# A two-layer trunk on one core: forget gates turned to rows of heads, an earlier load of decay rows, and an output projection that begins among the last attention units

## The chip, the core and the metric

The kernel runs on one core of one Trainium2 chip. The metric is the device time of one execution in microseconds, as the median of several runs. Five engines work side by side and are kept in step by semaphores that the program sets and waits for: TensorE (matrix products and transposes), VectorE, ScalarE, GpSimd (POOL) and SyncE (SP). SP, ScalarE and GpSimd also issue transfers, each from a queue of its own in the order of its program.

## What is computed

The input is 512 positions of width 1024 in float32. There are two layers. The change touches the part between them and the attention of the second one:

```python
def shared_kv(x_kv, kv_norm, kv_w, kv_b_f, k_norm):
    h = rmsnorm(x_kv, kv_norm)
    kvf = h @ kv_w                       # 1024 -> 1024 keys, 1024 values, 16 forget logits
    k, v, f = jnp.split(kvf, [D_MODEL, 2 * D_MODEL], axis=-1)
    k = rmsnorm(k.reshape(B, S, N_HEADS, HEAD_DIM), k_norm)
    v = v.reshape(B, S, N_HEADS, HEAD_DIM)
    log_f = jax.nn.log_sigmoid((f + kv_b_f).astype(jnp.float32))
    cum = jnp.cumsum(log_f, axis=1).transpose(0, 2, 1)
    return k, v, cum

def forgetting_attention(h, k, v, cum, w_qg, q_norm, w_out):
    q, gate = jnp.split(h @ w_qg, 2, axis=-1)
    q = rmsnorm(q.reshape(B, S, N_HEADS, HEAD_DIM), q_norm)
    # per block of 128 queries: scores q k^T * scale + cum[query] - cum[key], causal, softmax, times v
    return (o * jax.nn.sigmoid(gate)) @ w_out
```

There are 16 heads of width 64. Before this stands layer 0 (a gated mixer and a mixture of 32 experts), after it the second mixture of 32 experts, whose weights (6 MB each) stream in from memory.

## The kernel before

**Order of the work.** The second half of the program runs: normalised rows "kv" are turned and split; key projection (G_K, 8 groups); forget logits; value projection (G_VV, 8 groups); rows "b" are turned; cumulative sums; query projection (G_Q, 8 groups); 32 attention units (8 pairs of heads times 4 blocks of 128 queries); output projection (G_WO, 8 groups); router; mixture of experts (`moe_pe`, `moe_dve`, `moe_act`, `moe_loads`). Each engine has its own program, written out by hand, and runs it strictly in order.

**Products.** A float32 value is written as the sum of two rounded parts, hi and lo. `split_product` makes three matmuls of 128 x 128 by 512: hi x hi, hi x lo, lo x hi (L1203, L1204, L1205 of the profile). A group is 8 blocks of the inner dimension, so 24 matmuls, accumulated in one of the banks `ps[0]` and `ps[1]` in turn. A weight tile is loaded by SP (`load_tile`, which waits until the tile two before has been used), its hi part is made by ScalarE (L583), its lo part by VectorE (L795), four pieces each. Products of plain float32 operands are made without splitting; the profile shows two matmul instructions for each of those, and one for a transpose.

**Forget logits.** For each block of 128 positions, each of 8 inner blocks and both parts, two plain float32 products with 64 stationary columns and 16 moving ones (L1520). VectorE adds the bias (L1103), ScalarE makes log-sigmoid from it, VectorE joins the pieces (L1116). The layout is positions on partitions, `lf[128, 4 * 16]`.

**Cumulative sums.** Ten products of 16 moving columns with a triangle or ones as stationary operand (L1535, L1536), copied by VectorE (L1125), turned to 16 rows of heads by four transposes (L1540), negated by ScalarE and stored to memory as `ncum_rows`.

**Decay rows.** In the scores, each unit needs the row of its head on all 128 partitions. ScalarE loads them in pairs (`load_nck`, L713) from `ncum_rows` into two slots of `nck`, the first two when the last query block has been written (`kn_out` 16). VectorE adds them to the scores and takes the maximum in one instruction (L1147).

**Attention units.** In turn `u` TensorE makes the scores of unit u (L1557, mask L1560) into banks 2 * (u % 2) and the next, a slice of the gate projection (L1572, which for the first pair waits for a sum that VectorE makes, L1137), the product with values of the pair that is complete (L1585, once in four units, 3 units late), and the transposes of the probabilities of unit u - 2 (L1596). VectorE copies these out (L1166, ScalarE the other head, L744), and after the product with values it applies the gate and splits the result (L1172 to L1174). Units 32 to 34 of the loop only finish what is begun.

**Output projection.** It waits for the gated result of all 8 pairs, then makes 8 groups: n = 0, 1 (512 output columns each) by t = 0 to 3. Group g uses bank g % 2; from the third on it waits for VectorE's addition of group g - 2 (`x_attn`, L1180). VectorE's order is: add group 0, split the second weight tile, add group 1, and so on. SP loads expert weights as groups end: three parts after the last product with values, two after group 4, four after group 8.

Of the kernel before, what the change touches and what calls it, by code (L numbers as in the profile page):

```python
# [24 lines left out]
P = 128  # L25
D = 1024
T = 512
# [30 lines left out]
def trunk(nc, x_in, a_norm, a_w_in, a_b_in, a_v_norm, a_w_s, a_b_s, a_w_out, kv_norm, kv_w, kv_b_f, k_norm,  # L58
          b_norm, b_w_qg, q_norm, b_w_out, m_norm, m_w_group, m_b_group, m_w_expert, m_b_expert,
          m_w1, m_w3, m_w2, out):  # L60
    with ExitStack() as ctx:
# [68 lines left out]
        nck = scr(6 * COL, 10 * COL).rearrange("p (b h n) -> p b h n", b=2, h=2)  # L130
# [59 lines left out]
        cols_raw = sb("cols_raw", [N_COLS, P])  # L190
# [5 lines left out]
        wf = sb("wf", [P, KD, HEADS])  # L196
# [88 lines left out]
        kn_out = sem("kn_out")  # L285
        f_done = sem("f_done")
        f_ready = sem("f_ready")
# [3 lines left out]
        cum_ready = sem("cum_ready")  # L291
        cumT_done = sem("cumT_done")
        ncum_ready = sem("ncum_ready")
        ncum_stored = sem("ncum_stored")
        nck_loaded = sems("nck_loaded", 2)
        s_done = sem("s_done")
# [140 lines left out]
        def _(pool):  # L437
# [105 lines left out]

            item_tables(1)

        @block.scalar
        def _(act):
# [150 lines left out]
            head_norms(0, G_K, 0, KT, {0: T_K + 1, 5: T_VV})  # L698
            act.wait_ge(f_ready, 1)
# [3 lines left out]
            split_tile(T_VV + 1)  # L703
            split_tile(T_Q)
            transposed_rows("b")
            act.wait_ge(cumT_done, 1)
# [4 lines left out]
            def load_nck(c):  # L711
                for h in range(2):
                    act.dma_start(nck[:, c % 2, h, :], ncum_rows[2 * c + h].partition_broadcast(P))\  # L713
# [5 lines left out]
            load_nck(0)  # L719
# [31 lines left out]
        def _(dve):  # L751
# [262 lines left out]

            dve.wait_ge(small_loaded, 32)
# [65 lines left out]
            def head_norms(r, g0, splits):  # L1081
                for j in range(8):
# [13 lines left out]
                    if j in splits:  # L1096
# [4 lines left out]
            dve.wait_ge(f_done, 1)  # L1101
            f3 = lf[:, 0, :].rearrange("p (t n) -> p t n", t=NT)
            v.tensor_tensor(f3, ps[6][:, 0:NT * HEADS].rearrange("p (t n) -> p t n", t=NT),  # L1103
                            over_t(bf_bc[:, :], HEADS), ALU.add).then_inc(f_ready, 1)
            dve.wait_ge(f_ready, 1)
            then(v.tensor_scalar(lf[:, 2, :], lf[:, 0, :], 0.0, None, ALU.min))
            for j in range(8):
# [6 lines left out]
                if j == 3:  # L1114
# [15 lines left out]
            for u in range(n_units + 4):  # L1130
                if u < n_units:
# [7 lines left out]
                    if i == 0:  # L1139
                        dve.wait_ge(nck_loaded[c % 2], 32 * (c // 2 + 1))  # L1140
                    for h in range(2):
                        dve.wait_ge(s_done, 2 * u + h + 1)
                        if u >= 3:
# [4 lines left out]
                                               in1=nck[:, c % 2, h, 0:w], scale=-1.0, scalar=BIG, op0=ALU.add,  # L1148
# [44 lines left out]
        def _(pe):  # L1193
# [75 lines left out]
            def project(i, g0, bank_free):  # L1269

                for t in range(NT):
# [5 lines left out]
                    last.then_inc(acc_ready, 1)  # L1277

# [151 lines left out]
            nc.tensor.transpose(ps[6][:, 0:N_COLS], cols_raw[:, :], ident[0:N_COLS, 0:N_COLS])\  # L1430
# [94 lines left out]
            project(T_VV, G_VV, free_vv)  # L1525
# [112 lines left out]
```

## Time and profile before

| | us |
|---|---|
| median of 3 runs | 1659.6 |
| lowest and highest | 1659.26 and 1671.69 |
| span of the profiled execution, first to last instruction | 1656.1 |
| TensorE busy (share of the span) | 1513.8 (91%) |
| VectorE busy | 982.5 (59%) |
| ScalarE busy | 458.7 (28%) |
| GpSimd busy | 24.7 (1%) |

The page gives busy time by engine, the granted TensorE clock in slices of the span (1.00 is 2.4 GHz, 0.50 is 1.2 GHz), the costliest groups of instructions, the transfers, and the chain of work that ended last, followed back from the last instruction. TensorE's busy time is no measure of how much it does: a product at the lower clock is busy about twice as long.

### The profile page before, as it was taken

What the parts mean: (1) busy time and instruction counts of PE and PEld (TensorE: products, weight loads), DVE (VectorE), ACT (ScalarE), POOL (GpSimd) and SP (SyncE); (2) the same over time, 40 slices, a digit from 0 to 9 for tenths busy, and PEclk for the clock granted to TensorE, in tenths of its full rate; (3) what the DMA queues carried; (4) which work ended last, traced back from release to release, by engine and by line L of the source; (5) the groups of instructions that cost most, each with busy time, mean ns of one, the idle gap of its engine ahead of it and who ended that gap; (6) DMA issues with size and microseconds to landing.
All of it is one profiled execution on the core that took longest, in us unless ns stands there. A gap on an engine that the chain in (4) does not pass through costs nothing.

```text
span 1656.1 us, 45993 instructions
## 1 busy us (share of the span) xinstructions
PE 1513.8 (91%) x19125; PEld 1019.5 (62%) x19126; DVE 982.5 (59%) x2067; ACT 458.7 (28%) x757; POOL 24.7 (1%) x61
## 2 busy tenths in 40 slices
PE   8999999998999899977899989989999999977667
PEld 7888888755555555544787844457655555543334
DVE  5337642576776677745625346651776777754446
ACT  5442321422222122211541334433221222211111
POOL 2100000100000000000000000000000000000000
PEclk9999999999999999988989999999999999998888
DMA  5421224889999999999122121143899997999995
GB/s 206 131 102 51 102 102 152 332 361 411 418 415 425 429 429 404 431 427 390 35 81 95 59 89 56 60 191 126 363 412 427 424 402 299 404 426 428 429 429 211
DMA packets 55787, 462.17 MB, mean 279 GB/s; under 512 B 4433, under 2 KB 4561, under 8 KB 31153
## 3 DMA queue, kind: packets, MB, share of 16 engines
q1 hardware_dynamic: 51680, 453.00, 66.6%
q10 hardware_dynamic: 2480, 4.75, 0.9%
q0 software_dynamic: 1568, 3.59, 0.7%
q8 instruction: 44, 0.72, 0.2%
q14 instruction: 15, 0.11, 0.0%
HBM read 459.19 MB, written 2.13 MB: 279 GB/s over the span
## 4 chain that ended last, share of the span: by engine, by line
PE 60%; DMA 33%; DVE 4%; issue 1%; SPq 1%; ACT 0%; DVEq 0%; ACTq 0%
DMA EB<-in_m_w 32%; PE ps L1345 10%; PE ps L1203 9%; PE ps L1205 9%; PE ps L1204 9%; PE ps L1334 5%; PE ps L1355 4%; PE ps L1317 3%; PE ps L1572 3%; PE ps L1557 1%; PE ps L1585 1%; PE ps L1596 1%; PE ps L1444 1%; DVE EB_r L795 1%; SPq L384 1%
## 5 line engine op out<-in xcount | busy, mean ns | idle before, releaser
L1345 PE MATMUL ps<-EB,SCR 128*32 128x256 f32 x6016 | 378.4, 408 | 95.1 <-DMA EB<-in_m_w 81.6
L1345 PEld LDWEIGHTS ps<-EB,SCR 128*32 128x32 f32 x6016 | 200.7, 117 | 265.1 <-issue 144.1
L914 DVE TENSOR_TENSOR X<-X,ps 128x1024 f32 x188 | 221.1, 1218 | 28.1 <-PE ps L1317 28.1
L1205 PE MATMUL ps<-EB_r 128*128 128x512 f32 x512 | 201.7, 394 | 0.0
L1334 PE MATMUL ps<-H,SCR 128*32 128x256 f32 x3072 | 185.7, 382 | 0.0
L906 DVE TENSOR_TENSOR SCR<-SCR,ps 128x128 f32<-128x128 f32 x94 | 37.2, 395 | 248.4 <-ACT SCR L621 248.3
L1355 PE MATMUL ps<-EB,SCR 128*32 128x256 f32 x3008 | 179.5, 379 | 0.0
L624 ACT ACTIVATE SCR_r<-ps,SCR 128x256 f32 x94 | 44.6, 474 | 445.4 <-PE ps L1355 445.4
L1355 PEld LDWEIGHTS ps<-EB,SCR 128*32 128x32 f32 x3008 | 97.8, 110 | 64.5
L1317 PEld LDWEIGHTS ps<-SCR_r 32*128 32x128 f32 x3136 | 101.4, 187 | 48.1 <-issue 44.5
L1203 PE MATMUL ps<-EB_r,H_r 128*128 128x512 f32 x320 | 127.9, 400 | 1.0 <-DVE EB L993 1.0
L1317 PE MATMUL ps<-SCR_r 32*128 32x256 f32 x3136 | 121.3, 292 | 8.0 <-DVE SCR_r L927 3.8
L1334 PEld LDWEIGHTS ps<-H,SCR 128*32 128x32 f32 x3072 | 90.0, 109 | 62.2
L1204 PE MATMUL ps<-EB_r,H_r 128*128 128x512 f32 x320 | 126.0, 394 | 0.0
L1204 PE MATMUL ps<-EB_r 128*128 128x512 f32 x320 | 125.2, 391 | 0.0
L621 ACT ACT_TABLE_LOAD x94 | 120.6, 1283 | 2.0 <-ACT SCR L617 0.3
L795 DVE TENSOR_TENSOR EB_r<-EB,EB_r 128x1024 fp32r<-128x1024 f32 x80 | 92.9, 1220 | 42.0 <-ACT EB_r L583 42.0
L1205 PEld LDWEIGHTS ps<-EB_r 128*128 128x128 f32 x512 | 97.2, 190 | 20.7
L621 ACT ACTIVATE SCR<-ps 128x128 f32<-128x128 f32 x94 | 26.1, 278 | 281.9 <-PE ps L1345 281.9
L583 ACT ACTIVATE EB_r<-EB 128x1024 fp32r<-128x1024 f32 x80 | 78.2, 1047 | 72.9 <-DMA EB<-in_a_w_out 41.8
L890 DVE SCALAR_TENSOR_TENSOR SCR_r<-SCR,item_slot,SCR_r 128x256 fp32r<-128x256 f32 x196 | 86.3, 482 | 15.4 <-DVE SCR_r L887 15.3
L1203 PE MATMUL ps<-EB_r 128*128 128x512 f32 x192 | 76.6, 399 | 2.0 <-DVE EB_r L1174 2.0
(233 smaller groups left out, 1643.6 us busy)
## 6 DMA issues: line engine op xcount, KB each, us to landing
EB<-in_m_w SPq DMA_DIRECT2D x192, 2048.0 KB, 9.9
EB<-in_a_w_in SPq DMA_DIRECT2D x8, 2048.0 KB, 9.0
EB<-in_a_w_out SPq DMA_DIRECT2D x4, 2048.0 KB, 7.8
EB<-in_kv_w SPq DMA_DIRECT2D x4, 2048.0 KB, 14.4
EB<-in_b_w_qg SPq DMA_DIRECT2D x4, 2048.0 KB, 8.9
SCR<-ncum_rows ACTq DMA_DIRECT2D x16, 256.0 KB, 3.7
EB<-in_b_w_out SPq DMA_DIRECT2D x2, 2048.0 KB, 9.4
X<-in_x SPq DMA_DIRECT2D x4, 512.0 KB, 7.0
```

What stands on the lines that cost most here:

```text
L583: a.activation(ring_hi[j][:, 2 * q:2 * q + 2, :], ring[j][:, 2 * q:2 * q + 2, :], ACT.Copy)\
L621: a.activation(silu, ps[0][:, 0:P], ACT.Silu).then_inc(m["silu"], 1)
L795: v.tensor_tensor(ring_lo[j][:, 2 * q:2 * q + 2, :], ring[j][:, 2 * q:2 * q + 2, :], ring_hi[j][:, 2 * q:2 * q + 2, :].bitcast(F32), ALU.s ...
L890: v.scalar_tensor_tensor(dst[:, i, :], toks[1], item_slot[:, bass.ds(items[i] + 2, 1)], dst[:, i, :].bitcast(F32), ALU.is_equal, ALU.add). ...
L914: add = v.tensor_tensor(X_t, X_t, moved[1][:, :, t, :], ALU.add)
L1203: mm(o, left[0], right[0], start=start, stop=False)
L1204: mm(o, left[0], right[1], start=False, stop=False)
L1205: return mm(o, left[1], right[0], start=False, stop=stop)
L1317: last = mm(moved[banks][:, g, t, :], sides[rows, i, t * P:(t + 1) * P], y_parts[rows, i, k, :], start=i == 0 and k == 0, stop=i == 1 and ...
L1334: last = mm(ps[1][g * CAP:(g + 1) * CAP, 0:CW], S[:, c, :], H[:, c * D + g * CW:c * D + (g + 1) * CW], start=c == 0, stop=c == NT - 1)
L1345: last = mm(ps[0][g * CAP:(g + 1) * CAP, 0:2 * P].rearrange("p (w n) -> p w n", w=2), xT[:, k, :], w13_sb[s][:, :, k, g * P:(g + 1) * P], ...
L1355: last = mm(ps[2][g * CAP:(g + 1) * CAP, CW:2 * CW], hidT[:, c, :], w2_sb[s][:, c, g * CW:(g + 1) * CW], start=c == 0, stop=c == KE - 1)
```

## The change

1. **Logits with heads on partitions.** Instead of 128 plain products with 16 moving columns, 24 split products with the 16 gate weights as stationary operand and all 512 positions as moving one. The gate weights are split once, early in layer 0 (ScalarE, VectorE). ScalarE copies the [16, 512] result out; TensorE turns it back to positions on partitions with four transposes after the second group of the value projection; VectorE adds the bias then, and joins the pieces after the fifth group rather than the fourth.
2. **Sums with heads on partitions.** The same ten products with the operands exchanged: the logs are the stationary operand (16 columns), the triangle or ones the moving one (128 columns). The result has heads on partitions at once; VectorE's copy, the four transposes and their semaphores are gone.
3. **First pair's decay rows.** GpSimd loads them into `gain`, after the sums are stored and the last rows "b" are written. ScalarE no longer loads them; the even slot of `nck` is now `gain` for all even pairs.
4. **Output projection.** In loop turns 32, 33 and 34 TensorE makes blocks 0 to 2, 3 to 5 and 6 of group 0; after the loop blocks 0 to 6 of group 1; then block 7 of both, and the other groups as before.

```diff
-        nck = scr(6 * COL, 10 * COL).rearrange("p (b h n) -> p b h n", b=2, h=2)
+        nck = [at.rearrange("p (h n) -> p h n", h=2) for at in (gain[:, :], scr(6 * COL, 8 * COL))]
...
+            pool.wait_ge(ncum_stored, 16)
+            pool.wait_ge(norm["b"]["hrow"], NT)
+            for h in range(2):
+                pool.dma_start(nck[0][:, h, :], ncum_rows[h].partition_broadcast(P)).then_inc(nck_first, 16)
+
             item_tables(1)
...
             act.wait_ge(wst_ready, 2)
+            act.wait_ge(col_loaded, 16 * N_COL_LOADS)
+            a.activation(wf_hi[:, :, :], wf[:, :, :], ACT.Copy).then_inc(wf_split, 1)
...
             head_norms(0, G_K, 0, KT, {0: T_K + 1, 5: T_VV})
+            act.wait_ge(f_done, 1)
+            a.activation(junk[0:HEADS, 0:T], ps[6][0:HEADS, :], ACT.Copy).then_inc(f_out, 1)
+            split_tile(T_VV + 1)
             act.wait_ge(f_ready, 1)
...
-            load_nck(0)
             load_nck(1)
...
+            dve.wait_ge(wf_split, 1)
+            v.tensor_tensor(wf_lo[:, :, :], wf[:, :, :], wf_hi[:, :, :].bitcast(F32), ALU.subtract).then_inc(wf_split, 1)
...
+                if j == 1:
+                    dve.wait_ge(f_turned, 1)
+                    v.tensor_tensor(f3, ps[7][:, 0:NT * HEADS].rearrange("p (t n) -> p t n", t=NT),
+                                    over_t(bf_bc[:, :], HEADS), ALU.add).then_inc(f_ready, 1)
+                    dve.wait_ge(f_ready, 1)
+                    then(v.tensor_scalar(lf[:, 2, :], lf[:, 0, :], 0.0, None, ALU.min))
+                if j == 4:
...
-            dve.wait_ge(cum_done, 1)
-            v.tensor_copy(lf[:, 1, :], ps[7][:, 0:NT * HEADS]).then_inc(cum_ready, 1)
...
-                        dve.wait_ge(nck_loaded[c % 2], 32 * (c // 2 + 1))
+                        dve.wait_ge(*((nck_loaded[c % 2], 32 * (c // 2 + c % 2)) if c else (nck_first, 32)))
...
-            for t in range(NT):
-                for k in range(KD):
-                    for part, h in enumerate(h_part(k, t)):
-                        for c in range(2):
-                            last = mm(ps[6][c * HALF:(c + 1) * HALF, t * HEADS:(t + 1) * HEADS],
-                                      h.bitcast(F32)[:, c * HALF:(c + 1) * HALF], wf[:, k, :],
-                                      start=k == 0 and part == 0, stop=k == KD - 1 and part == 1)
+            pe.wait_ge(wf_split, 2)
+            for k in range(KD):
+                last = split_product(ps[6][0:HEADS, :], (wf_hi[:, k, :], wf_lo[:, k, :]), h_part(k), k == 0, k == KD - 1)
             last.then_inc(f_done, 1)
+
+            def turn_forget():
+
+                pe.wait_ge(f_out, 1)
+                for t in range(NT):
+                    last = nc.tensor.transpose(ps[7][:, t * HEADS:(t + 1) * HEADS], junk[0:HEADS, t * P:(t + 1) * P],
+                                               ident[0:HEADS, 0:HEADS])
+                last.then_inc(f_turned, 1)
...
             pe.wait_ge(lf_ready, 1)
-            for c in range(NT):
-                o = ps[7][:, c * HEADS:(c + 1) * HEADS]
-                for b in range(c):
-                    mm(o, ones[:, :], lf[:, 0, b * HEADS:(b + 1) * HEADS], start=b == 0, stop=False)
-                last = mm(o, tri_in[:, :], lf[:, 0, c * HEADS:(c + 1) * HEADS], start=c == 0, stop=True)
+            for t in range(NT):
+                o = ps[6][0:HEADS, t * P:(t + 1) * P]
+                for b in range(t):
+                    mm(o, lf[:, 0, b * HEADS:(b + 1) * HEADS], ones[:, :], start=b == 0, stop=False)
+                last = mm(o, lf[:, 0, t * HEADS:(t + 1) * HEADS], tri_in[:, :], start=t == 0, stop=True)
             last.then_inc(cum_done, 1)
...
+            def attend_out(n, t, c0, c1):
+
+                i, g = T_WO + n, NT * n + t
+                if c0 == 0:
+                    pe.wait_ge(*((x_attn, g - 1) if g >= 2 else (s_max, 2 * (PAIRS * NT - 1))))
+                for c in range(c0, c1):
+                    if n == 0 and t == 0:
+                        pe.wait_ge(o_gated, c + 1)
+                    if n == 1:
+                        router_step(1, t, c)
+                    wait_split(i, c, t == 0)
+                    last = split_product(ps[g % 2][:, :], (GT_hi[:, c, t * P:(t + 1) * P], GT_lo[:, c, t * P:(t + 1) * P]),
+                                         w_part(i % 2, c), c == 0, c == PAIRS - 1)
+                if c1 == PAIRS:
+                    last.then_inc(acc_ready, 1)
...
+                if u >= n_units:
+                    attend_out(0, 0, 3 * (u - n_units), min(3 * (u - n_units) + 3, PAIRS - 1))
                 if 2 <= u < n_units + 2:
...
-            pe.wait_ge(o_gated, PAIRS)
...
+            attend_out(0, 1, 0, PAIRS - 1)
+            for t in range(2):
+                attend_out(0, t, PAIRS - 1, PAIRS)
+            for g in range(2, 2 * NT):
+                attend_out(g // NT, g % NT, 0, PAIRS)
             router_end(1)
```

## Rows read from the trace of the kernel before

**Rows 1.** The page: shares of the span in the chain that ended last.

```profile
PE 60%; DMA 33%; DVE 4%; issue 1%; SPq 1%; ACT 0%; DVEq 0%; ACTq 0%
```

**Rows 2.** Stretches: us, busy time by engine, then granted clock, DMA share, GB/s.

```profile
852.50:857.80 5.30, 5.30 (x105) 5.26 (x103) 0.00 (x0) 0.00 (x0) 0.00 (x0) 0.51 0.48 177
...
904.00:910.60 6.60, 4.11 (x33) 3.37 (x32) 5.97 (x8) 3.39 (x7) 0.00 (x0) 1.00 0.77 258
...
913.90:917.30 3.40, 3.40 (x10) 2.69 (x9) 0.00 (x0) 0.59 (x1) 0.00 (x0) 0.52 0.06 14
...
966.10:972.00 5.90, 5.85 (x16) 2.45 (x16) 0.02 (x1) 1.28 (x1) 0.00 (x0) 0.50 1.04 377
...
1099.00:1108.40 9.40, 7.38 (x26) 4.41 (x27) 1.81 (x3) 3.90 (x4) 0.00 (x0) 0.68 0.66 242
...
1128.20:1157.00 28.80, 28.46 (x217) 23.13 (x215) 5.89 (x13) 13.93 (x16) 0.00 (x0) 1.00 0.37 147
```

**Rows 3.** Timeline of TensorE, logits to value projection: start, us, line, count, [idle before].

```profile
847.88 0.29 PE L1520 MATMUL ps<-wf,H_r 128*64 128x16 f32 x4
...
857.76 1.12 PE L1479 MATMUL ps<-ident,SCR 128*128 128x128 f32 x4
858.53 0.78 PE L1203 MATMUL ps<-EB_r,H_r 128*128 128x512 f32 x1
...
862.91 0.40 PE L1204 MATMUL ps<-EB_r,H_r 128*128 128x512 f32 x1
```

**Rows 4.** Timeline of TensorE around the cumulative sums.

```profile
910.74 0.29 PE L1536 MATMUL ps<-lf,tri_in 128*128 128x16 f32 x2
...
913.36 0.60 PE L1540 MATMUL ps<-ident,lf 128*16 128x128 f32 x4 [0.32 <-DVE lf L1125]
913.72 0.49 PE L1203 MATMUL ps<-EB_r,H_r 128*128 128x512 f32 x1
```

**Rows 5.** Chain that ended last, at the first attention unit: start, us, what.

```profile
966.55 5.40 DMA SCR<-ncum_rows
```

**Rows 6.** Timeline of TensorE at the first two attention units.

```profile
971.88 0.36 PE L1560 MATMUL ps<-mask_b,ident_b 128*128 128x128 bf16 x2
973.68 0.70 PE L1572 MATMUL ps<-H,EB 128*128 128x512 f32 x1 [1.44 <-DVE H L1137]
```

**Rows 7.** Timeline of TensorE, last attention units and output projection.

```profile
1087.36 2.37 PE L1585 MATMUL ps<-EB 128*64 128x512 f32 x16
...
1092.98 0.60 PE L1596 MATMUL ps<-ident,SCR 128*128 128x128 f32 x4
1094.01 1.02 PE L1596 MATMUL ps<-ident,SCR 128*128 128x128 f32 x6 [0.42 <-DVE EB L1166]
1097.25 1.06 PE L1596 MATMUL ps<-ident,SCR 128*128 128x128 f32 x8 [2.22 <-DVE EB L1166]
1099.05 3.71 PE L1585 MATMUL ps<-EB 128*64 128x512 f32 x16 [0.73 <-DVE EB L1166]
1104.73 0.50 PE L1203 MATMUL ps<-EB_r 128*128 128x512 f32 x1 [1.97 <-DVE EB_r L1174]
...
1117.33 0.39 PE L1203 MATMUL ps<-EB_r 128*128 128x512 f32 x1
...
1128.21 0.39 PE L1203 MATMUL ps<-EB_r 128*128 128x512 f32 x1
```

**Rows 8.** Timeline of VectorE in the same stretch.

```profile
1096.56 0.55 DVE L1166 COPY EB<-ps 128x384 f32<-128x384 f32 x1
...
1112.09 0.69 DVE L1180 TENSOR_TENSOR X<-X,ps 128x512 f32<-128x512 f32 x1 [7.42 <-PE ps L1205]
1112.70 4.63 DVE L795 TENSOR_TENSOR EB_r<-EB,EB_r 128x1024 fp32r<-128x1024 f32 x4
```

**Rows 9.** Timeline of SP's queue during the output projection.

```profile
1128.40 28.61 SPq L370 DMA_DIRECT2D EB<-in_m_w  x3
```

**Rows 10.** Transfers by line: queue, count, KB each, median us to landing.

```profile
EB<-in_a_b_s POOLq DMA_DIRECT2D x1, 512.0 KB, 8.5
```

More of the change, by code:

```diff
@@ L189, in trunk @@
         eps = sb("eps", [P, 1])
-        cols_raw = sb("cols_raw", [N_COLS, P])
+        cols_raw, wf_hi_rows = sb_split("cols_raw", [P, P])
+        wf_hi = wf_hi_rows[:, :].rearrange("p (k n) -> p k n", k=KD)
         cols = sb("cols", [P, N_COLS])
@@ L195, in trunk @@
         gpk = sb("gpk", [P, 2, KD])
-        wf = sb("wf", [P, KD, HEADS])
+        wf, wf_lo = sb_split("wf", [P, KD, HEADS])
         bf_bc = sb("bf_bc", [P, HEADS])
@@ L285, in trunk @@
         kn_out = sem("kn_out")
+        wf_split = sem("wf_split")
         f_done = sem("f_done")
+        f_out = sem("f_out")
+        f_turned = sem("f_turned")
         f_ready = sem("f_ready")
@@ L295, in trunk @@
         nck_loaded = sems("nck_loaded", 2)
+        nck_first = sem("nck_first")
         s_done = sem("s_done")
@@ L1267, in router_end, with project @@
                 router_logits(l, NT - 1)
-            def project(i, g0, bank_free):
+            def project(i, g0, bank_free, between=None):
                 for t in range(NT):
@@ L1277, in project @@
                     last.then_inc(acc_ready, 1)
+                    if between is not None and t == 1:
+                        between()
             def project_transposed(i, g0, bank_free):
@@ L1531, in _ @@
             pe.wait_ge(lf_ready, 1)
-            for c in range(NT):
-                o = ps[7][:, c * HEADS:(c + 1) * HEADS]
-                for b in range(c):
-                    mm(o, ones[:, :], lf[:, 0, b * HEADS:(b + 1) * HEADS], start=b == 0, stop=False)
-                last = mm(o, tri_in[:, :], lf[:, 0, c * HEADS:(c + 1) * HEADS], start=c == 0, stop=True)
-            last.then_inc(cum_done, 1)
-            pe.wait_ge(cum_ready, 1)
-            for c in range(NT):
-                last = nc.tensor.transpose(ps[6][0:HEADS, c * P:(c + 1) * P], lf[:, 1, c * HEADS:(c + 1) * HEADS],
-                                           ident[:, :])
-            last.then_inc(cumT_done, 1)
+            for t in range(NT):
[3 more added lines that the diff above has]
+                last = mm(o, lf[:, 0, t * HEADS:(t + 1) * HEADS], tri_in[:, :], start=t == 0, stop=True)
+            last.then_inc(cum_done, 1)
             project_heads("b", T_Q, G_Q, 1, free_q)
             turn_heads(15)
+            def attend_out(n, t, c0, c1):
[12 more added lines that the diff above has]
+                    last.then_inc(acc_ready, 1)
             pe.wait_ge(kn_out, 16)
@@ L1598, in _ @@
                         last.then_inc(pt_tr, 1)
-            pe.wait_ge(o_gated, PAIRS)
-            for n in range(2):
-                i = T_WO + n
-                for t in range(NT):
-                    g = G_WO + 4 * n + t
-                    if 4 * n + t >= 2:
-                        pe.wait_ge(x_attn, 4 * n + t - 1)
-                    for c in range(PAIRS):
-                        if n == 1:
-                            router_step(1, t, c)
-                        wait_split(i, c, t == 0)
-                        last = split_product(ps[g % 2][:, :], (GT_hi[:, c, t * P:(t + 1) * P],
-                                                               GT_lo[:, c, t * P:(t + 1) * P]),
-                                             w_part(i % 2, c), c == 0, c == PAIRS - 1)
-                    last.then_inc(acc_ready, 1)
+            attend_out(0, 1, 0, PAIRS - 1)
[3 more added lines that the diff above has]
+                attend_out(g // NT, g % NT, 0, PAIRS)
             router_end(1)
```

19 lines of the change are left out of this document (5 added, 14 removed).

## The prediction

> **What bounds the kernel now.** I read the page's chain first. TensorE carries 60% of the span, transfers 33% [rows 1]; nearly all of the transfers are expert weights of the two mixture stages, which the change does not touch. So a microsecond counts where TensorE is the chain, and I read the stretches that the diff names in the order of time: granted clock by stretch, then TensorE's own timeline around each. The reader is to see four places. The forget logits, 256 narrow instructions, run without a pause, yet during them the granted clock falls from full to the lower level, 1.2 GHz, and stays there into the value projection [rows 2, 3]. Around the sums over positions TensorE waits a little, and the query projection starts at the lower clock [rows 2, 4]. At the first attention unit the chain holds 5.40 us of the decay rows' transfer, and TensorE stands 1.44 us behind VectorE [rows 5, 6]. At the last units it stands 0.42, 2.22, 0.73 and 1.97 us, and its clock is down again until 1108.4, when ten products of the output projection are through [rows 2, 7].
>
> Does time won there reach the end? The next expert loads wait in SP's queue for TensorE: the three SP issues of 1128.40 stretch over 28.61 us, since the last of them waits for the last projection group, and the transfer engines are 0.37 busy from 1128.2 to 1157.0 [rows 2, 9]. The weights of the second mixture stage are thus asked for when the projection is done, not when a full queue lets them, and everything behind it moves as one.
>
> A full-clock product of 512 columns costs 0.227 us here: 48 of them lie between 1117.33 and 1128.21 [rows 7].
>
> **Forget logits.** From their first instruction (847.88) to the eleventh product of the value projection (862.91) pass 15.03 us [rows 3]: 256 narrow instructions, one turn of key heads (857.76 to 858.53) and ten products at the lower clock (858.53 to 862.91). After: three products for each of 8 blocks, 24 x 0.227 = 5.44; the turn at twice the clock, half of 0.77 = 0.39; ten products at full clock, 2.27; and, two groups on, four transposes back, at the 0.115 of a narrow instruction below, 0.46. That makes 8.56, a gain of **6.5**. I take the cost of a 16-wide stationary block as that of a 128-wide one, which is the dearer neighbour; no row has it for a 512-column product. What is queued behind: ScalarE copies the logits out and splits the next weight tile, whose load was issued in time; VectorE waits for the turned logits after the second value group, TensorE does not want its next split before the fifth, 2 x 5.44 us later. The new split of the gate weights (one small instruction on ScalarE, one on VectorE, in the first layer) is taken at nothing: TensorE is then inside a group of 24 products, 5.4 us, and only wants VectorE's next result two groups on. Uncovered it would cost under 1 us. Bounds for this part: 6.5, or less 3.3 if the clock falls all the same (below).
>
> **Sums over positions.** Before, the first product starts at 910.74, TensorE waits 0.32 us at 913.36 for VectorE's copy, does four transposes, and the query projection starts at 913.72: 2.98 us [rows 4]. The 20 instructions until that wait took 913.36 - 0.32 - 910.74 = 2.30, or 0.115 each. After, 20 instructions with the operands exchanged, no copy, no transposes: 2.30. Each moves 128 columns instead of 16, and loads 16 instead of 128; I price them alike. Gain 0.68. From 913.9 to 917.3 the products ran at 0.52 of the clock; the same work at full clock is done in half the 3.4 us. Is that 1.7 won? At 904 to 910.6 TensorE was busy only 4.11 of 6.6 us with transposes of 128 columns and kept a clock of 1.00; both falls, here and at 852.5, came behind runs of 16-column instructions [rows 2, 3, 4], and neither run remains. I take it: together **2.4**, bounds 0.7 and 2.4.
>
> The Trainium skill (TensorE: Matmul & The Clock Gate, Part 1: The HAM clock gate) has the clock go down after the array was idle. By it this 1.7 would stay lost, for the pauses between 904 and 910.6 remain, and the sum would come out 1.7 us less. The trace does not agree at the forget logits, where the clock fell to 0.51 with TensorE busy 5.30 of 5.30 us [rows 2].
>
> **First decay rows.** Before, ScalarE asks for them only when queries are done. After, GpSimd's queue asks as soon as the sums are stored. The slowest small load on that queue in this trace took 8.5 us [rows 10]; two in a row would be there 17 us after 914, by 931, and the first reader wants them at 967. The cover is the whole query projection, some 36 us. What is won is not 5.40: VectorE is freed 4 to 5 us earlier, but TensorE, at the lower clock (0.50 from 966.1 to 972), has own work until 972.2, and stood only 1.44 us for VectorE before 973.68 [rows 2, 6]. After that TensorE sets the pace of the units. Gain **1.4**. Bounds: 0, if VectorE is late for another reason; 3, if the clock rises sooner. The GpSimd issue is behind nothing and its next customer is the mixture stage. The slot in `gain` is free once the last normalised rows of "b" are written, before 910.
>
> **Projection among the last units.** I lay it out from the rows [rows 7, 8]. TensorE is free at about 1093.5. Nine products (blocks 0 to 2 of group 0): 2.04, to 1095.55. Six transposes, which began at 1094.01 before, now end at about 1096.2; VectorE takes them at 1096.56 as before, because it is busy with other work until then. So nothing is lost here. Nine products (blocks 3 to 5), to 1098.25; the last eight transposes thus start 1.0 later than at 1097.25. From there to the last value products it was 1.80, so these start at 1100.05, at full clock now since no pause over 0.8 is left, and take 2.3 (the same sixteen at 1087.36), to 1102.35; before, 1102.76. Then 3 + 21 products, 5.44, to 1107.8; VectorE's gate of the last pair, 1.97 after the value products, is ready at 1104.3 and hidden. Six more products, 1.36, to 1109.15.
>
> Here the change adds a wait: the third group needs the bank of the first, and group 0 ends only three products before group 1. Its last product is out at 1108.65, VectorE's addition takes 0.69 (1112.09), so the third group starts at 1109.4, 0.25 late. Behind that addition VectorE splits the last weight tile, 4.63, and only then adds group 1: 1114.7. The fourth group wants that at 1109.4 + 5.44 = 1114.85. It just fits; were it late, each tenth counts. Two groups more, 10.88: the fifth starts at 1120.3 instead of 1128.21, a gain of **7.9**. Bounds: 4.5 if the clock falls as before (1.4 on the value products, ten products at 0.2 more each), 8.2 without the new wait.
>
> **Sum.** 6.5 + 2.4 + 1.4 + 7.9 = 18.2 us. The profiled execution spans 1656.1 us; that gives 1637.9. The median of the runs is 1659.6, 3.5 more, which lies around the span and stays. Forecast **1641.4 us**.
>
> **Rivals.**
> 1. *The clock falls under the new product as well.* Only 16 columns of the array hold weights, and no row shows such a run. If it fell after 4.6 us as now (847.88 to 852.5), four products cost 0.2 more each, the turn 0.39 and ten products 2.1: 3.3 us. With the 1.7 of the sums: 18.2 - 5.0 = 13.2, 1646.4 us; with the last units at the lower clock too (3.4 us) 1649.8. For it: the falls of [rows 2]. Against: 512-column products come without a pause.
> 2. *Only the query projection starts slow.* For it the 2.5 us of pauses before 910.6; against it the 1.00 held through them. 18.2 - 1.7 = 16.5, 1643.1 us. This is what the skill's rule above gives.
> 3. *The expert loads do not come sooner.* If transfers in flight were the limit behind the projection, most of the gain would be given back: about 1656. Against it the 0.37 of [rows 2].
> 4. *Slower: GpSimd's loads are late.* One wait, VectorE's for the first pair. Up to 967.4 a late landing costs nothing, until about 972 it eats the 1.4, from there each microsecond costs one; with the other gains (16.8) the kernel is slower than before once they land after about 989, over 70 us after their issue, against 8.5 seen. Landing at 995 they would make it 1659.6 - 16.8 + 23 = 1666 us.
> 5. *Luck with the clock.* It rises sooner at the first units: 1637 to 1639 us.
>
> The Trainium skill (SBUF — State Buffer, SBUF: two separate sides) warns that GpSimd cannot write its descriptors while VectorE runs certain copies within SBUF. It speaks for rival 4; no row shows such a delay, and I have no price for it beyond the 8.5 us.
>
> **How the numbers follow.** The forecast 0.50, with its own range of 1639.5 to 1643.5; rival 1 0.20, rival 2 0.15, rival 3 0.04, rival 4 0.03, rival 5 0.08. Leaving out 3 and 4 and the far ends of 1 and 5, the range is 1638 to 1649. A change of 1%, 16.6 us, is about what a measurement of this kernel tells from none; the border is 1643.0. Below it lie four fifths of the forecast (0.40), half of rival 2 (0.08) and rival 5 (0.08): faster 0.56. Slower is rival 4: 0.03. Within 1%: 0.41.
>
> **What would show it.** Right: the logits as 24 products over 5.4 us, clock 1.0 through the value projection's start; the query projection at 0.227 from its first products; VectorE's first reduction about 0.5 us behind the mask product, released by TensorE; the fifth output group some 18 us earlier; a wait of about 0.25 us ahead of the third. Wrong: a clock of 0.5 in any of the first three, a load of `gain` from GpSimd as what ends VectorE's wait, a long wait of TensorE for VectorE's addition in the fourth group, or the wait for expert weights after 1186 longer by what was won.

## The result, and the profile after

The changed kernel takes 1638.15 us (median of four runs, 1635.26 to 1647.78), the kernel before 1661.55 in the same rounds (1659.26 to 1671.69): a ratio of 0.9871, with an interval from 0.9837 to 0.9905. In later rounds it took 1641.18 us (1637.96 to 1645.70, six runs) against 1658.22 (1651.81 to 1664.53, eleven runs), 0.9906 [0.9879, 0.9932]. Faster, then, by 1.3% in the first rounds and 0.9% in the second, about 20 us in the mean of the two differences (23.4 and 17.0). Executions of one kernel lie up to 12.5 us apart in the first rounds, which matters for everything below.

The profiled execution spans 1636.7 us, 19.4 less than that of before. The four places, in the order of time. Stretches of the kernel after, as in [rows 2] (length, busy time of TensorE, its weight loads, VectorE, ScalarE and GpSimd, then granted clock, transfer share, GB/s):

```profile
848.70:855.03 6.33, 6.33 (x34) 3.10 (x32) 1.58 (x3) 1.48 (x3) 0.00 (x0) 1.00 0.80 263
855.03:859.50 4.47, 4.47 (x23) 3.68 (x22) 0.00 (x0) 3.72 (x5) 0.00 (x0) 1.00 0.27 97
899.30:908.20 8.90, 6.41 (x53) 5.20 (x51) 8.02 (x12) 4.33 (x8) 0.00 (x0) 1.00 0.69 238
908.20:911.00 2.80, 2.80 (x14) 2.27 (x13) 0.00 (x0) 0.59 (x1) 0.15 (x1) 1.00 0.05 12
959.10:965.00 5.90, 5.87 (x16) 2.46 (x17) 1.65 (x5) 2.16 (x5) 0.00 (x0) 0.50 0.81 296
1084.50:1093.90 9.40, 8.67 (x54) 6.48 (x52) 4.74 (x11) 3.97 (x8) 0.00 (x0) 1.00 0.62 225
1093.90:1101.00 7.10, 7.05 (x31) 5.51 (x30) 2.50 (x5) 2.44 (x3) 0.00 (x0) 1.00 0.88 330
1101.00:1112.30 11.30, 11.25 (x50) 9.31 (x51) 5.86 (x7) 0.00 (x0) 0.00 (x0) 1.00 0.82 349
```

The clock is 1.00 at the logits and into the value projection (before 0.51), at the start of the query projection (before 0.52) and at the last units (before 0.68). Only the first attention unit still runs at 0.50.

The timeline of TensorE in the kernel after, at the same places (start, length, line, count, idle time before it):

```profile
849.06 0.48 PE L1214 MATMUL ps<-H_r,cols_raw_r 128*16 128x512 f32 x1
...
854.67 0.60 PE L1492 MATMUL ps<-ident,SCR 128*128 128x128 f32 x4
855.03 0.48 PE L1214 MATMUL ps<-EB_r,H_r 128*128 128x512 f32 x1
...
905.96 0.39 PE L1554 MATMUL ps<-tri_in,lf 128*16 128x128 f32 x2
...
908.25 0.50 PE L1214 MATMUL ps<-EB_r,H_r 128*128 128x512 f32 x1
...
964.86 0.39 PE L1589 MATMUL ps<-mask_b,ident_b 128*128 128x128 bf16 x2
965.05 2.15 PE L1601 MATMUL ps<-H,EB 128*128 128x512 f32 x4
...
1091.56 2.37 PE L1614 MATMUL ps<-EB 128*64 128x512 f32 x16 [0.73 <-DVE EB L1177]
...
1100.56 0.39 PE L1216 MATMUL ps<-EB_r 128*128 128x512 f32 x1
1101.05 0.50 PE L1214 MATMUL ps<-EB_r 128*128 128x512 f32 x1
```

The logits are 24 products from 849.06 to 854.67, 5.61 us, where 256 instructions had taken 9.88 [rows 3]. The sums go from 905.96 to 908.25, 2.29 us against 2.98 [rows 4]. Ahead of the second unit there is no pause where 1.44 stood [rows 6]. The waits of 0.42, 2.22 and 1.97 at the end are gone [rows 7]; 0.73 is left, and the new wait stands ahead of the third output group: the last product is issued at 1100.56 and runs for some 0.23, the next starts at 1101.05.

VectorE and GpSimd at the first decay rows, and VectorE and SP at the output projection, in the kernel after:

```profile
910.85 1.07 POOL L550 DMA_DIRECT2D gain<-ncum_rows  x2 [104.42 <-DMA ncum_rows<-SCR]
...
960.30 0.29 DVE L1158 CUSTOM_DVE_ANT_0 SCR<-ps,gain 128x128 f32<-128x128 f32 x1 [1.53 <-PE ps L1589]
...
1100.31 0.69 DVE L1191 TENSOR_TENSOR X<-X,ps 128x512 f32<-128x512 f32 x1 [4.47 <-PE ps L1216]
1100.92 4.62 DVE L806 TENSOR_TENSOR EB_r<-EB,EB_r 128x1024 fp32r<-128x1024 f32 x4
1105.46 0.68 DVE L1191 TENSOR_TENSOR X<-X,ps 128x512 f32<-128x512 f32 x1
...
1112.26 28.64 SPq L373 DMA_DIRECT2D EB<-in_m_w  x3
```

The loads were asked for at 910.85 and the transfer list gives them 3.4 us each; VectorE's first reduction waits for TensorE, not for them. The weights of the second mixture are asked for at 1112.26, 16.14 earlier than in [rows 9].

### The profile page after: what moved, and what is told of

It is laid out like the page before. It is cut to its first block, busy times and chain, and to the rows that moved or that the text cites. A ratio compares the mean times of both kernels' runs of the same rounds, so it can differ in the third digit from the quotient of the medians.

```text
span 1636.7 us, 45535 instructions
## 1 busy us (share of the span) xinstructions
PE 1499.2 (92%) x18893; PEld 1007.2 (62%) x18894; DVE 982.1 (60%) x2067; ACT 459.3 (28%) x759; POOL 25.8 (2%) x63
## 3 DMA queue, kind: packets, MB, share of 16 engines
q10 hardware_dynamic: 2192, 4.23, 0.8%
## 4 chain that ended last, share of the span: by engine, by line
PE 67%; DMA 26%; DVE 4%; issue 1%; SPq 0%; ACT 0%; DVEq 0%
DMA EB<-in_m_w 26%; PE ps L1358 12%; PE ps L1214 9%; PE ps L1216 9%; PE ps L1215 9%; PE ps L1347 6%; PE ps L1368 6%; PE ps L1330 4%; PE ps L1601 3%; PE ps L1586 1%; PE ps L1614 1%; PE ps L1627 1%; PE ps L1210 1%; PE ps L1457 1%; PE ps L1237 1%
## 5 line engine op out<-in xcount | busy, mean ns | idle before, releaser
L925 DVE TENSOR_TENSOR X<-X,ps 128x1024 f32 x188 | 221.1, 1218 | 28.7 <-PE ps L1330 28.7
```

The lines of the kernel that those rows point to most:

```text
L925: add = v.tensor_tensor(X_t, X_t, moved[1][:, :, t, :], ALU.add)
```

## The trace cut into stretches

One execution against another hides a term of 2 us under a spread of 8. So each profile was cut at instructions that all kernels have, and the lengths compared, in us:

- **A**: turn of key heads ahead of the logits, to the first transposes of the rows of "b"
- **B**: from there to the tenth product of the query projection
- **C**: first scores of the first attention unit to those of the fifth
- **D**: transposes behind the scores of the last unit, to SP's issue behind the fourth output group
- **start** is what lies before A, **end** the second mixture behind the last output group. Their code is the same in all, but for the small split of the gate weights

| kernel | start | A | B | C | D | end |
|---|---|---|---|---|---|---|
| before | 847.35 | 56.83 | 13.25 | 16.32 | 35.42 | 499.04 |
| after | 848.70 | 50.60 | 11.14 | 14.88 | 27.73 | 495.77 |
| a_logits | 847.51 | 50.60 | 12.97 | 18.83 | 32.49 | 496.02 |
| b_sums | 844.20 | 55.30 | 11.12 | 18.36 | 37.61 | 497.64 |
| c_rows | 845.78 | 56.83 | 16.17 | 14.23 | 35.65 | 501.26 |
| d_out | 848.22 | 56.82 | 16.11 | 17.91 | 27.74 | 494.95 |
| undo_sums | 843.55 | 50.60 | 14.68 | 14.60 | 27.74 | 499.61 |
| undo_decay | 848.58 | 50.60 | 11.11 | 19.57 | 27.74 | 497.13 |
| tail_fill | 850.44 | 55.27 | 15.99 | 18.66 | 34.49 | 496.34 |
| fill_wide | 849.40 | 50.60 | 11.12 | 11.92 | 27.73 | 496.56 |
| fill_narrow | 843.39 | 50.60 | 11.11 | 14.47 | 27.74 | 499.65 |
| before_again | 855.37 | 55.27 | 16.01 | 18.15 | 35.63 | 499.36 |
| after_again | 845.72 | 50.60 | 11.14 | 14.40 | 27.74 | 498.41 |
| fill_wide_again | 845.04 | 50.60 | 11.14 | 11.91 | 27.74 | 499.78 |

In the pair of profiles the local gains are 6.23 (A), 2.11 (B), 1.44 (C) and 7.69 (D), 17.5 in all. The start and the end of the same code vary by 12.0 and 6.3 us over the table: the rest of the 19.4 is the end, 3.27 shorter, less 1.35 of a later start. The end is no shorter with the earlier projection in the mean (497.7 us over the eight profiles that have it, 498.3 over the six others), so both are put down to the spread between executions. What lies between the stretches differs little: 48.7 to 49.2 us from B to C, 110.5 from C to D (111.1 in c_rows), 28.7 from D to the end.

## Each part alone

The kernel before with one part of the change each, three rounds beside the kernel before (1659.86 us, 1652.16 to 1672.81, 31 runs).

**a_logits**, the logits as rows of heads (the lines of code shown here and below are shortened):

```diff
-for t, k, part, c: mm(ps[6][...], h[...], wf[:, k, :])
+for k in range(KD):
+    last = split_product(ps[6][0:HEADS, :], (wf_hi[:, k, :], wf_lo[:, k, :]), h_part(k), ...)
```

> The kernel before with the first part alone: split product for the forget logits, turned back after the second value group. Theory (by content): the stretch from the turn ahead of the logits to the first transposes of the rows b falls from 56.8 us to 50.6, the clock stays at 1.00 through the start of the value projection, and the query projection still starts at about half the clock, because the sums are the old narrow ones. Rival (luck): the clock falls under the 16-wide product in this execution, the stretch is 53 to 54 us. Whole kernel: 6.2 us less than before.

Measured 1652.72 us (1648.42 to 1665.17, 10 runs), 0.9974 [0.9944, 1.0003]. A is 50.60, and the value projection starts at full clock. The query projection still starts at the lower clock, as expected (0.50 from 908.4 to 911.7).

**b_sums**, the sums with exchanged operands, without copy and transposes:

```diff
-mm(o, tri_in[:, :], lf[:, 0, c * HEADS:(c + 1) * HEADS], ...)
+mm(o, lf[:, 0, t * HEADS:(t + 1) * HEADS], tri_in[:, :], ...)
```

> The kernel before with the exchanged operands of the cumulative sums alone. Theory (the old clock falls come from runs of 16-column instructions): the old logits lose the clock again, at about 4.6 us from their start; the query projection starts at full clock, the stretch from the transposes of rows b to the tenth query product goes from 13.25 us to 11.1. Rival (the Trainium skill, TensorE: Matmul & The Clock Gate, Part 1: The HAM clock gate: the clock goes down after idleness, and the pauses among the transposes remain): that start stays slow, 12.6 us. Whole kernel: 2.1 us less, or 0.7.

Measured 1656.05 us (1653.53 to 1662.42), 0.9974 [0.9950, 0.9999]. B is 11.12, and the clock is 1.00 at the start of the query projection, though the logits are still narrow and brought it down in A, some 6 us behind their start rather than the 4.6 expected. The clock was at 1.00 through the transposes too, in this one profile, so the rival of the expectation did not come true.

**c_rows**, the first pair's decay rows loaded by GpSimd into `gain`:

```diff
-            load_nck(0)
+pool.dma_start(nck[0][:, h, :], ncum_rows[h].partition_broadcast(P)).then_inc(nck_first, 16)
```

> The kernel before with the first decay rows loaded by GpSimd into gain alone. Theory: VectorE starts its first reduction 4.6 us sooner, but from the first scores to those of the fifth unit only 1.4 us are won, 16.3 to 14.9, as TensorE's own work at the lower clock takes the place. Rival: the whole 4 to 5 us, 11.5. Whole kernel: 1.4 us less.

Measured 1657.59 us (1647.25 to 1663.62), 0.9979 [0.9949, 1.0010]. C is 14.23, where 14.9 was expected, and VectorE's first reduction starts 1.17 us behind the first scores instead of 5.83.

**d_out**, the output projection among the last units:

```diff
+                if u >= n_units:
+                    attend_out(0, 0, 3 * (u - n_units), min(3 * (u - n_units) + 3, PAIRS - 1))
```

> The kernel before with the earlier output projection alone. Theory: from the transposes of unit 29 to the issue behind the fourth output group 35.4 us become 27.7, clock 1.00 throughout, 0.25 us of wait ahead of the third group. Rival: the gain depends on the other parts (their clock), less than 5 us here. Whole kernel: 7.7 us less, and the mixture stage behind it as long as before (499.0) within what it varies by.

Measured 1650.89 us (1647.38 to 1656.25), 0.9941 [0.9918, 0.9963]. D is 27.74.

By medians the four give 7.1, 3.8, 2.3 and 9.0 us, 22.2 together, which agrees with the 23.4 and 17.0 of the whole within what times of whole executions leave open. The whole-kernel times can't rank them, and for a_logits and c_rows they don't even establish a gain, since the intervals reach past 1. The stretches can: each part brings its own stretch to the same length with and without the others, so none needs another. A part in its new form takes the same time in every profile, to 0.03 us in A, B and D. In its old form it does not, and that is the finding that the next sections follow.

## What the profile of before had shown cheaply

**undo_sums**, the changed kernel with the old sums, one execution:

```diff
-mm(o, lf[:, 0, t * HEADS:(t + 1) * HEADS], tri_in[:, :], ...)
+mm(o, tri_in[:, :], lf[:, 0, c * HEADS:(c + 1) * HEADS], ...)
```

> The changed kernel with the cumulative sums alone put back (narrow instructions, VectorE's copy, four transposes). Theory: from the transposes of rows b to the tenth query product 11.1 us go back to 12.8 to 13.3, with the clock near half behind the sums. Rival (the falls were chance): the clock stays at 1.00 and it is 11.8.

Measured 1640.57 us, B 14.68: 3.5 more than the changed kernel's, where the profile of before had shown only 2.1 more, and past the 12.8 to 13.3 that were expected. The clock is 1.00 up to 901.9 and 0.50 from there to 905.0; the first narrow sum had begun at 900.72.

**undo_decay**, the changed kernel with the old load of the first pair's rows, one execution:

```diff
-                        dve.wait_ge(*(... if c else (nck_first, 32)))
+                        dve.wait_ge(nck_loaded[c % 2], 32 * (c // 2 + 1))
+            load_nck(0)
```

> The changed kernel with the first pair's decay rows loaded as before, by ScalarE behind the query heads. Theory 1 (the late rows make a pause that also brings the clock down a second time): first to fifth unit 17 to 19 us against 14.2 to 14.9, VectorE waits for the transfer 5 to 6.6 us, time about 1641. Theory 2 (only the 1.44 us pause of the first profile): 16.0 to 16.4 us, time about 1640.

Measured 1644.60 us, C 19.57, 4.7 to 5.3 more than with the early load and a little more than the 17 to 19 of theory 1. Its TensorE and VectorE at the first units:

```profile
963.76 1.14 PE L1581 MATMUL ps<-EB 64*128 64x256 f32 x4
964.83 0.29 PE L1584 MATMUL ps<-mask_b,ident_b 128*128 128x128 bf16 x2
968.45 3.48 PE L1596 MATMUL ps<-H,EB 128*128 128x512 f32 x4 [3.33 <-DVE H L1143]
971.87 0.92 PE L1581 MATMUL ps<-EB 64*128 64x384 f32 x4
...
972.84 1.94 PE L1596 MATMUL ps<-H,EB 128*128 128x512 f32 x4
...
966.75 0.29 DVE L1153 CUSTOM_DVE_ANT_0 SCR<-ps,SCR 128x128 f32<-128x128 f32 x1 [8.13 <-DMA SCR<-ncum_rows]
```

VectorE waits 8.13 us for the rows (5 to 6.6 expected), TensorE stands 3.33 for VectorE. The four products behind that pause take 3.48 us, the same four a little later 1.94. The clock had risen by 965 and went down a second time:

```profile
959.20:962.00 2.80, 2.80 (x9) 1.55 (x10) 0.00 (x0) 0.96 (x1) 0.00 (x0) 0.50 1.02 390
962.00:966.00 4.00, 3.12 (x9) 0.88 (x7) 0.00 (x0) 0.33 (x1) 0.00 (x0) 0.66 0.72 257
966.00:970.00 4.00, 1.55 (x2) 0.84 (x3) 3.21 (x13) 1.97 (x8) 0.00 (x0) 0.76 0.03 13
970.00:974.00 4.00, 4.00 (x12) 1.39 (x11) 1.83 (x6) 0.42 (x1) 0.00 (x0) 0.81 0.00 0
974.00:978.70 4.70, 4.57 (x18) 1.87 (x16) 4.25 (x15) 2.88 (x10) 0.00 (x0) 1.00 0.03 3
```

So late rows cost a pause and a second spell at 1.2 GHz. In the profile of before the pause was 1.44 and no second spell came; in the five other profiles with the old load the pause was 1.83 to 3.06 and a second spell came each time.

**before_again**, the kernel before once more, nothing edited:

> The kernel before once more, for a second set of stretches. Theory 1 (the profile of before shown first has by chance short stretches behind the sums and at the first units): sums to tenth query product about 15 to 16 us against 13.25, first to fifth unit about 18 against 16.32. Theory 2 (those two are what this kernel always takes, and only the kernels with one part changed differ): 13.25 and 16.32 within 0.3.

Measured 1669.96 us, span 1668.1. B is 16.01 and C 18.15 against 13.25 and 16.32. Its last transposes and first sum, its stretches around the sums, and those at the first units:

```profile
916.20 1.94 PE L1226 MATMUL ps<-ident,SCR 128*128 128x128 f32 x8 [1.23 <-DVE EB_r L787]
917.94 0.45 PE L1536 MATMUL ps<-lf,tri_in 128*128 128x16 f32 x2
...
910.60:914.00 3.40, 2.13 (x19) 1.89 (x18) 2.91 (x4) 2.06 (x4) 0.00 (x0) 1.00 0.56 140
914.00:918.00 4.00, 2.77 (x17) 2.45 (x16) 3.89 (x7) 1.73 (x3) 0.00 (x0) 0.71 1.03 395
918.00:922.20 4.20, 4.20 (x21) 4.12 (x20) 1.34 (x2) 0.60 (x1) 0.00 (x0) 0.50 0.03 11
...
979.00:983.00 4.00, 2.38 (x8) 0.48 (x6) 1.18 (x5) 0.85 (x4) 0.00 (x0) 0.80 0.68 216
983.00:987.00 4.00, 3.48 (x6) 1.16 (x8) 2.85 (x9) 1.12 (x5) 0.00 (x0) 0.62 0.00 0
```

Here too the clock goes down a second time in C (0.80, then 0.62). And in B it was down before the first 16-column sum was issued, among the transposes with their pauses of 1.27 and 1.23. The prediction laid the fall in B to the narrow sums; this one came without them.

**after_again**, the changed kernel once more, nothing edited:

> The changed kernel as it is, timed in more rounds beside the next one. Expected: 1638 us, span 1635 to 1640; turn ahead of the logits to the first transposes of rows b 50.60, those to the tenth query product 11.1, first unit to fifth 14.2 to 14.9, transposes of the last unit but two to the issue of the next weights 27.73. If the new stretches only happened to be alike so far, one of them comes out over 0.5 us apart.

Measured as told at the top, span 1636.2: 50.60, 11.14, 14.40, 27.74. The new stretches hold.

Mean lengths over all profiles with a stretch in its old and in its new form:

| | old form | new form | gain | predicted |
|---|---|---|---|---|
| A | 56.05 (6 profiles, 55.27 to 56.83) | 50.60 (8) | 5.5 | 6.5 |
| B | 15.03 (7, 12.97 to 16.17) | 11.13 (7) | 3.9 | 2.4 |
| C | 18.26 (7, 16.32 to 19.57) | 14.52 (5, 14.23 to 14.88) | 3.7 | 1.4 |
| D | 35.36 (5, 32.49 to 37.61) | 27.74 (8) | 7.6 | 7.9 |

(C in its new form counts fill_narrow and leaves out the kernels with wide fillers; D in its old form leaves out tail_fill.) The sum is 20.7 us, in agreement with the 23.4 and 17.0 of the medians.

## What the clock is worth at the last units

**tail_fill**, the kernel before with 16 unread instructions of 128 columns in each of two of the pauses, one execution:

```diff
+                if u >= n_units:
+                    keep_busy(0, (8, 8, 0)[u - n_units])
```

> The kernel before, with 8 products of 128 x 128 by 128 columns that nobody reads put into the loop turns 32 and 33, where the change puts its output products; the output projection itself is left where it was. It shows the part of the gain that is only clock. Theory: the last product with values takes 2.4 us instead of 3.7 and the output projection starts at full clock, so that the stretch of 35.4 us loses 3.3, 32.1; the other 4.4 of the 7.7 are work moved into pauses. Rival: the fillers hold up the transposes and nothing is won, 35 or more.

Measured 1661.33 us, D 34.49, only 0.9 under the mean of the old form: neither the 32.1 of the theory nor the 35 of the rival. Its TensorE, at the value products and the start of the output projection:

```profile
1106.43 2.38 PE L1585 MATMUL ps<-EB 128*64 128x512 f32 x16 [0.73 <-DVE EB L1166]
1110.77 0.50 PE L1203 MATMUL ps<-EB_r 128*128 128x512 f32 x1 [1.97 <-DVE EB_r L1174]
```

Its stretches, before and behind that start:

```profile
1099.00:1110.00 11.00, 9.07 (x69) 7.05 (x67) 6.77 (x18) 5.12 (x10) 0.00 (x0) 1.00 0.62 203
1110.77:1115.00 4.23, 4.23 (x13) 3.32 (x14) 0.00 (x0) 1.36 (x2) 0.00 (x0) 0.66 0.95 407
```

The value products take 2.38 instead of 3.71 [rows 7], and the clock was at full up to there. That the fillers held it is not shown by one execution, since a_logits below holds it there without any. And the wait of 1.97 for the gate of the last pair is still empty, and behind it the clock goes down, with 0.66 over the first 4.23 us of the output projection. So 1.33 us was saved at the value products, nothing behind them, and 0.4 of it went into the fillers (from the transposes to the value products 6.44 us against 6.07).

The old form gives a cleaner split by itself. In a_logits the clock happened to stay at full through the same pauses, and D is 32.49; in b_sums it was down through the value products, and D is 37.61:

```profile
1095.49 2.38 PE L1603 MATMUL ps<-EB 128*64 128x512 f32 x16 [0.73 <-DVE EB L1176]
1099.84 0.50 PE L1213 MATMUL ps<-EB_r 128*128 128x512 f32 x1 [1.97 <-DVE EB_r L1184]
```

```profile
1094.31 4.53 PE L1576 MATMUL ps<-EB 128*64 128x512 f32 x16 [0.73 <-DVE EB L1162]
1100.81 0.80 PE L1199 MATMUL ps<-EB_r 128*128 128x512 f32 x1 [1.97 <-DVE EB_r L1170]
```

(The first fence is a_logits, the second b_sums.) Against 27.74 the pauses alone are worth 32.49 - 27.74 = 4.75 us, and the clock from 0 to 5.1 more, 2.9 in the mean.

## Holding the clock at the first units

One place is left at 0.50 in the kernel after, so two kernels fill the pauses around the last turn of query heads with 26 unread instructions (18919 of TensorE in both, 18893 in the kernel after).

**fill_wide**, instructions of 128 columns, three rounds:

```diff
+            keep_busy(7, 10)
             turn_heads(15)
+            keep_busy(7, 3)
```

> The changed kernel with unread products of 128 columns in the two pauses of TensorE ahead of the first attention unit (10 ahead of the last turn of query heads, 3 behind it). Theory: these pauses are what loses the clock; with them filled the first units run at 1.00, the first four slices of the gate projection take 1.9 us instead of 3.7, and 1 to 3 us are won up to the fifth unit (14.9 becomes 12 to 14; VectorE's sum ahead of each slice is next to bind). Rival: the fillers delay the chain to the first scores by what they save.

**fill_narrow**, the same with 16 moving columns, one execution:

```diff
-mm(ps[bank][:, at:at + P], tri[:, :], tri_in[:, :], start=True, stop=True)
+mm(ps[bank][:, 0:HEADS], tri[:, :], tri_in[:, 0:HEADS], start=True, stop=True)
```

> As the one before, with 16 moving columns in the fillers in place of 128; each instruction should last as long, since its weights are loaded as before (0.11 us). Theory (runs of 16-column instructions lose the clock though TensorE is never idle): the first units run at half the clock as in the changed kernel. Rival (only idle time counts): they run at 1.00 as with the wide fillers.

Stretches of fill_wide up to the first units, then the ten fillers and the stretches of fill_narrow:

```profile
955.00:959.80 4.80, 4.67 (x37) 4.11 (x36) 2.71 (x4) 2.16 (x4) 0.00 (x0) 1.00 0.56 180
959.80:966.60 6.80, 6.79 (x28) 2.98 (x29) 4.76 (x16) 3.29 (x10) 0.00 (x0) 1.00 0.69 259
```

```profile
949.92 2.30 PE L1215 MATMUL ps<-tri_in,tri 128*128 128x16 f32 x20
...
950.00:952.00 2.00, 2.00 (x21) 2.00 (x20) 1.28 (x3) 1.16 (x3) 0.00 (x0) 1.00 0.46 97
952.00:954.10 2.10, 1.97 (x13) 1.87 (x12) 1.43 (x2) 0.69 (x1) 0.00 (x0) 0.68 1.03 401
954.10:957.50 3.40, 3.40 (x10) 1.85 (x11) 1.65 (x5) 2.16 (x5) 0.00 (x0) 0.50 1.06 378
```

With the wide ones the clock stays at 1.00 and C is 11.92, 2.6 under the mean of the new form. With the narrow ones TensorE is as busy (3.97 of 4.10 us up to 954.1), yet the clock goes down and C is 14.47. The fillers fill the pauses in both: 20 instructions last 2.30 us with 16 columns and 2.40 with 128. All twelve profiles without wide fillers lose the clock here, that of fill_narrow among them, and neither of the two with them does. So in this place the width of the fillers decides it and not whether TensorE has a pause; for the narrow ones that rests on one execution.

fill_wide took 1641.79 us (1636.93 to 1651.21, six runs), 0.9903 [0.9859, 0.9947], fill_narrow 1637.01: against the 1638.15 of the changed kernel that says nothing about 2.6 us. So fill_wide was run once more, in the same rounds as the changed kernel. (The fillers are thirteen plain products of two instructions each; the expectation calls them triples by mistake.)

**fill_wide_again**, nothing edited:

> The changed kernel with thirteen unread 128-column product triples around the last turn of query heads, ahead of the first attention unit, now on the same chip and in the same rounds as the changed kernel alone. Theory 1 (the clock is held, the stretch from the first to the fifth unit is 2.3 to 3.0 us shorter, and this reaches the end): 1635.5 us, about 0.998 of the changed kernel alone. Theory 2 (the fillers cost as much elsewhere, or the chip takes the clock back later): 1638 to 1642, no better than the changed kernel.

Measured 1635.26 us (1633.80 to 1647.19, six runs), 0.9879 [0.9846, 0.9912], against 1641.18 (1637.96 to 1645.70) for the changed kernel. Five of its six runs lie below the lowest of the other, and C is 11.91 again. This is the fastest kernel of the study, and the likeliest worth is 2.6 to 2.9 us: from the tenth query product to the fifth unit, pauses and fillers included, the kernels with early rows take 63.4 to 63.6 us and both with wide fillers 60.6, and nothing behind C takes it back up to the next weights. It is not established by the times: over both sets of rounds its runs reach from 1633.80 to 1651.21 and those of the changed kernel from 1635.26 to 1647.78.

## Why the prediction was right, and by how much by luck

**Forecast.** 1641.4 us against 1638.15 and 1641.18, inside the range of 1638 to 1649 both times, though the first of them by 0.15 us only. The gain of 18.2 stands between the 23.4 and the 17.0 of the two sets of rounds.

**Logits, 6.5.** In the pair of profiles 6.23, in the mean 5.5. Steps confirmed: 24 products at 0.23 (5.61 us), the turn at 0.36, the first value products at 0.23; a 16-wide stationary block costs what a 128-wide one does. Rival 1 is out: clock 1.00 in all eight profiles with the new product. The term was a little large because the old form varies: in three of the six it took 55.27 to 55.30 instead of 56.83. The split of the gate weights in the first layer, taken at nothing, shows no cost in the start (846.5 us in the mean of the eight profiles that have it, 848.6 without), but a spread of 12 us would hide one.

**Sums, 2.4.** In the pair 2.11, of which 0.69 is work, as worked out, and 1.4 clock; in the mean 3.9, so 3.2 is clock. The size was read from one execution with a cheap spell. The reason given, that both falls "came behind runs of 16-column instructions", is right for part of the profiles only. All seven with the old sums lose the clock in B. In before, a_logits and undo_sums it goes down behind the start of the sums; B is 13.6 in their mean, 2.5 more than in the new form, near the 2.4 of the forecast. In c_rows, d_out, tail_fill and before_again it goes down 5.0 to 5.5 us behind the first transposes, where old and new code are the same, and is low when the first sum is issued; B is 16.0 to 16.2. So 2.5 is what can be laid to the sums with the runs at hand; that the rest of the 3.9 comes from them too is not shown. Rival 2, that the pauses between 904 and 910.6 would still bring it down, did not come true in any of the seven profiles with the new sums, but the clock does go down among them in those four.

The Trainium skill (TensorE: Matmul & The Clock Gate, Part 1: The HAM clock gate) lets the clock go down after the array was idle. Before_again at 914 to 918 (pauses of 1.27 and 1.23 us), undo_decay (3.33) and tail_fill (1.97) go that way; the logits [rows 2] and fill_narrow do not, since there it goes down with hardly a pause. Idle time alone does not decide it either: the kernel after has the same 1.27 and 1.23 among its transposes at 1.00, and a_logits passes the waits of the last units at 1.00.

What stays open is why the fall among the transposes came in four of five profiles with both old logits and old sums and in none of the nine others. Before and before_again are the same kernel and differ in it, so chance has a part.

**Decay rows, 1.4.** In the pair 1.44, in the mean 3.7, past the upper bound of 3. The step that failed is that only the 1.44 us for which TensorE stood are won: the pause is 1.44 to 3.33 in other executions of the same code, and behind the longer ones the clock goes down again, so that four instructions of the gate projection take up to 3.7 us (3.48 in undo_decay) against 1.94. Rival 4 is out, with loads that land in 3.4 us. That VectorE could hold up GpSimd's issue is not tested here, for VectorE had nothing to do from 907.78 to 914.74, when the issue came at 910.85.

**Output projection, 7.9.** In the pair 7.69, in the mean 7.6. The wait ahead of the third group is 0.26 against 0.25, the value products take 2.37 against 2.3. The addition of group 1 is through at 1105.46 + 0.68 = 1106.14, and the fourth group, 24 products behind 1101.05, starts at 1106.62 and does not wait for it. The forecast's own split, 4.5 without the clock, is 4.75.

**Reaching the end.** The reading of SP's queue was right: the next weights are asked for 16.14 us earlier, and the second mixture does not give it back (495.77 and 498.41 against 499.04 and 499.36). Rival 3 is out.

The sum of the four terms was 18.2, that of the pair of profiles 17.5, that of the means 20.7. Two terms too small by 1.5 and 2.3, one too large by 1.0: the forecast was near because such errors are small beside the whole, not because each price was known.

## What to carry to other kernels

Price a stretch from more than one execution when the clock falls in it: its old form can cost 3 us more or less, and one profile shows one throw. A pause of TensorE can be worth more than its length, since a spell at the lower clock may follow it; and to fill some pauses of a stretch can be too little, for the clock may go down behind one that is left (tail_fill). Cut traces at instructions that both kernels have: stretches of 10 to 50 us resolved tenths, where times of whole executions left 5 us open.

## What the runs showed of the hardware

- Where the clock does not change, a stretch of 50 us repeats to 0.01 us over eight profiles on several chips (A: 50.60 in each). Nearly all of the spread in the four stretches comes with the granted clock.
- The instructions of the sums take nearly the same with 16 moving and 128 stationary columns as the other way round, at full clock: from the first of them to the last pair (18 instructions) 1.93 us before and 1.98 after.
- TensorE without a pause does not by itself keep the full clock: 16-column instructions back to back ran into 0.51 at the logits and 0.68, then 0.50, in fill_narrow, where 128-column ones in the same place stayed at 1.00.
